# Moving 14 of 93 convolution taps on VectorE to later slots of a hybrid decoder layer

## The chip, the cores and the metric

The kernel runs on one core of a Trainium2 chip. The metric is the device time of one execution in microseconds (us); lower is better. The core has five engines that run side by side and meet only through semaphores: TensorE (PE in the rows, with its weight loads as PEld), VectorE (DVE), ScalarE (ACT), GpSimd (POOL) and SyncE (SP), which issues DMAs.

## The reference

Two layers of a decoder trunk work on 520 tokens: a prompt of 512 and eight decode tokens with state. Each layer has four token mixers beside each other, merged by sigmoid gates, and then a SwiGLU channel mixer:

```
xn = RMSNorm(x)
[A | B | C | D | gates] = xn @ w_in
A: o_a = Bg * dwconv3(Cg * h)
B: o_b = swish(LN(dwconv31(GLU(a, b))))        <- the 31-tap depthwise convolution
C: sliding-window attention (window 128) with QK-norm, rotary and sinks
D: gated linear attention, chunked recurrence
x = x + (sum_r sigmoid(gate_r) * (o_r @ w_branch[r])) @ w_out
x = x + SwiGLU(RMSNorm(x))
```

What matters here is branch B: each of 512 channels is convolved along the tokens with its own 31 weights. The sum for a channel is y[t] = bias + sum over w of weight[w] * u[t + w - 30].

## The kernel before, in words

**Layout.** Channels lie on the 128 partitions and tokens along the free dimension, so 512 channels are four chunks of 128 partitions by 520 tokens. Each fp32 product is made of three fp32r products: every weight tile and every activation tile is split into a rounded part (`whi`, `xhi`, by ScalarE) and the rest (`wlo`, `xlo`, by VectorE), and TensorE adds hi*hi, hi*lo and lo*hi in PSUM.

**Slots.** The input projection, the gates and the branch projections are 103 slots a layer, listed in order in `SLOTS`; a slot makes one output chunk. Those that matter here are numbered from 0:

- 0 to 7: `cfb` and `cfa`, the two inputs of the GLU of branch B. After slot 7 the convolution's input `cfu` is complete.
- 8 to 13: `aq` (four chunks of q), `ak`, `av`, each followed by norm and rotary steps two and four slots later.
- 14 to 25: branch A, as two groups of six: `sch` 14, 15; `scc` 16, 17; `scb` 18, 19; then `sch` 20, 21; `scc` 22, 23; `scb` 24, 25. An `scc` slot holds the whole short convolution of a chunk on VectorE (a chain of nine instructions behind the eviction, each waiting for those before it).
- 26 to 29: the first gates; 30 to 33 the first branch projection, and so on.

The accumulators `acc` are two buffers in turn: the products of slot n + 2 start only when VectorE has taken slot n out of PSUM.

**Order on VectorE.** It runs one fixed program. For each slot n the loop (see below) emits: `side(n)`, the attention or other small work hung on this slot; the `wlo` parts of the weight tiles up to slot n + 2 (line 1269); `evac(n, ...)`, the eviction of the accumulator times `rstd` (line 1260) and, in an `scc` slot, the short convolution (lines 1263, 1556, 1557); and then as many convolution taps as the table `TAPS_AT` gives for n. A tap is one SCALAR_TENSOR_TENSOR of 128 by 512, `cacc <- cfu * weight + cacc` (line 1263). VectorE does chunks 0 to 2, 93 taps: first chunks 0 and 1 in turn, then chunk 2. Since the program is in order, a tap in slot n delays all that VectorE does later: `side(n+1)`, `wlo`, and the eviction of n + 1.

**GpSimd** does chunk 3 by itself from the end of slot 7 on: for each tap a TENSOR_SCALAR into `ssum` (line 1723) and a TENSOR_TENSOR that adds it to `cacc` (line 1726).

**The attention steps on this stretch.** TensorE's own side work follows the products of its slot. At slot 17 (`SATT`) it makes the decode tokens' scores (line 663) from `qz`, which VectorE fills in its `side(17)` (line 1340). At slot 19 it transposes the probabilities `sprob` (line 669), which VectorE finishes in `side(19)` (line 1355) after ScalarE's exponential. The prompt's attention is in eight groups, started at slots `ATT` = 20, 22, 24, 26, 32, ...: scores on TensorE at the end of that slot (line 698), mask and maximum on VectorE in the next slot's side, exponentials on ScalarE, normalisation `prob` on VectorE in the side of the slot after (line 1260), and the transposes of `prob` on TensorE at the end of that slot (line 711), then the values (line 687). So group 1 has its scores in slot 22, its maximum in `side(23)`, its normalisation in `side(24)` and its transposes behind the products of slot 24.

Of the kernel before, what the change touches and what calls it, by code (L numbers as in the profile page):

```python
# [160 lines left out]
TAPS = [(c, w) for w in range(W2) for c in (0, 1)] + [(2, w) for w in range(W2)]  # L161
TAPS_AT = {}
_left = len(TAPS)
for _first, _last, _m in ((4, 7, 3), (8, 9, 4), (10, 17, 2), (20, 21, 2), (29, 29, 2), (30, 33, 1), (34, 37, 2),
                          (38, 41, 1), (42, 53, 3)):
    for _n in range(_first, _last + 1):
        TAPS_AT[_n] = min(_m, _left)
        _left -= TAPS_AT[_n]
# [1729 lines left out]
```

How the kernel before makes its waits and increments, by code:

```python
            def need(self, *points):  # L510
                for name, value in points:
                    self.eng.wait_ge(s[name], value)
# [3 lines left out]
            @block.sync  # L516
            def _(sp):
                for k in range(0, KD, 2):
                    sp.dma_start(x[:, k:k + 2], xt[:, k:k + 2]).then_inc(x_part[k // 2], 16)
                sp.dma_start(raw[:, 0], wt[0]).then_inc(raw_in[0], 16)
                sp.dma_start(raw[:, 1], wt[1]).then_inc(raw_in[1], 16)
                sp.dma_start(cs[:], cst).then_inc(cst_in, 16)
                sp.dma_start(glam[:], glam_d).then_inc(cst_in, 16)
                sp.dma_start(scanm[:], scan_d).then_inc(cst_in, 16)
                sp.dma_start(yt, xt).then_inc(y_out, 16)
                sp.wait_ge(raw_in[1], 16)
# [1 line left out]
            @block.scalar  # L529
            def _(a):
                a.dma_start(gmix[:], gm[0]).then_inc(s["gm_in"], 16)
                a.preload_act_table_set("natural_log_exp_and_others")
                a.wait_ge(s["gm_in"], 16)
                for k in range(KD):
                    if k % 2 == 0:
                        a.wait_ge(x_part[k // 2], 16)
                    nc.scalar.activation(xhi[:, k], x[:, k], ACT.Copy, scale=gmix[:, k:k + 1])\
                        .then_inc(s["xhi_done"], 1)
                    if k >= 2:
                        a.wait_ge(s["ss_done"], k - 1)
                    nc.scalar.activation(tmp[:, k % 2], x[:, k], ACT.Square).then_inc(s["ss_sq"], 1)
                a.wait_ge(raw_in[0], 16)
```

## Time and profile before

| | |
|---|---|
| time, three runs | 2087.36, 2087.77 (median), 2089.17 us |
| the profiled execution | 2088.41 us, of which 2086.4 us are the span from its first to its last instruction |
| mean granted TensorE clock | 0.994 of 2.4 GHz |
| PE, DVE, ACT, POOL busy | 98%, 59%, 38%, 18% of the span |
| slots 8 to 24 of layer 1 | 75.17 to 191.81 us (eviction of 8 to eviction of 24) |
| the same of layer 2 | 1109.34 to 1227.90 us |

The busy share of PE is an upper bound: a matmul that waits for its weights or is pipelined behind another counts as busy. A row of the timeline gives start, duration, engine, line, operation, what it writes and reads, the count when equal ones are merged, and in brackets the idle time before it and who ended it. Two taps that are merged have one start and the sum of their time.

### The profile page before, as it was taken

What the parts mean: (1) busy time and instruction counts of PE and PEld (TensorE: products, weight loads), DVE (VectorE), ACT (ScalarE), POOL (GpSimd) and SP (SyncE); (2) the same over time, 40 slices, a digit from 0 to 9 for tenths busy, and PEclk for the clock granted to TensorE, in tenths of its full rate; (3) what the DMA queues carried; (4) which work ended last, traced back from release to release, by engine and by line L of the source; (5) the groups of instructions that cost most, each with busy time, mean ns of one, the idle gap of its engine ahead of it and who ended that gap; (6) DMA issues with size and microseconds to landing.
All of it is one profiled execution on the core that took longest, in us unless ns stands there. A gap on an engine that the chain in (4) does not pass through costs nothing.

```text
span 2086.4 us, 38895 instructions
## 1 busy us (share of the span) xinstructions
PE 2036.1 (98%) x16516; PEld 1982.0 (95%) x16516; DVE 1225.7 (59%) x1667; ACT 787.3 (38%) x1209; POOL 380.6 (18%) x238
## 2 busy tenths in 40 slices
PE   6989999999999999999989999999999999999998
PEld 6989889999999999999989998899999999999998
DVE  4897667765556453345539975677555565533445
ACT  4323442643543432233233144435535333322332
POOL 0695000211104000000307930003111030000003
PEclk9999999999999999999999999999999999999999
DMA  7523323123222222222444243222223232222223
GB/s 237 97 84 82 71 72 109 67 92 102 105 99 85 98 95 89 99 81 78 139 120 88 91 62 82 73 100 82 94 82 122 82 101 101 75 93 95 101 76 127
DMA packets 70038, 199.54 MB, mean 96 GB/s; under 512 B 41554, under 2 KB 42706, under 8 KB 51408
## 3 DMA queue, kind: packets, MB, share of 16 engines
q1 hardware_dynamic: 26144, 177.50, 25.6%
q10 hardware_dynamic: 43760, 20.11, 5.4%
q8 instruction: 102, 1.67, 0.4%
q14 instruction: 32, 0.26, 0.0%
HBM read 187.42 MB, written 12.29 MB: 96 GB/s over the span
## 4 chain that ended last, share of the span: by engine, by line
PE 43%; DVE 5%; issue 1%; ACT 1%; POOL 0%; DVEq 0%; POOLq 0%
PE acc L604 40%; DVE cacc L1263 1%; DVE wlo L1269 1%; PE m L698 1%; PE m L687 1%; DVE q L1260 1%; ACT tmp L947 0%; DVE sct L1263 0%; PE m L711 0%; PE m L618 0%; DVE gt L1260 0%; PE m L813 0%; PE m L785 0%; PE m L823 0%; PE m L663 0%
## 5 line engine op out<-in xcount | busy, mean ns | idle before, releaser
L604 PE MATMUL acc<-xhi,wlo 128*128 128x260 f32 x3680 | 754.5, 286 | 28.7 <-PEq L567 19.5
L604 PE MATMUL acc<-xhi,whi 128*128 128x260 f32 x3680 | 743.8, 284 | 0.0
L604 PE MATMUL acc<-xlo,whi 128*128 128x260 f32 x3680 | 742.7, 283 | 0.0
L604 PEld LDWEIGHTS acc<-xhi,wlo 128*128 128x128 f32 x3680 | 571.7, 190 | 46.3 <-issue 40.0
L604 PEld LDWEIGHTS acc<-xhi,whi 128*128 128x128 f32 x3680 | 569.6, 189 | 0.0
L604 PEld LDWEIGHTS acc<-xlo,whi 128*128 128x128 f32 x3680 | 569.3, 189 | 0.0
L1269 DVE TENSOR_TENSOR wlo<-raw,whi 128x1024 fp32r<-128x1024 f32 (+3 forms) x344 | 434.4, 1271 | 36.2 <-ACT whi L964 34.8
L964 ACT ACTIVATE whi<-raw 128x1024 fp32r<-128x1024 f32 (+3 forms) x344 | 332.1, 994 | 255.2 <-PE acc L604 197.9
L947 ACT ACTIVATE gt<-gt 128x520 f32<-128x520 f32 x226 | 144.4, 639 | 215.0 <-DVE gt L1260 210.2
L1260 DVE TENSOR_TENSOR gt<-acc,rstd 128x520 f32<-128x520 f32 x80 | 55.9, 699 | 216.0 <-PE acc L604 195.7
L604 PE MATMUL acc<-hhi,whi 128*128 128x260 f32 x704 | 141.5, 282 | 0.0
L604 PE MATMUL acc<-hlo,whi 128*128 128x260 f32 x704 | 141.5, 282 | 0.0
L604 PE MATMUL acc<-hhi,wlo 128*128 128x260 f32 x704 | 141.4, 282 | 0.0
L1263 DVE SCALAR_TENSOR_TENSOR cacc<-cfu,pr,cacc 128x512 f32<-128x512 f32 x180 | 138.2, 794 | 1.6
L1767 POOL TENSOR_TENSOR tmp<-x 128x520 f32<-128x520 f32 x2 | 2.1, 1054 | 656.0 <-DVE x L1686 656.0
L1723 POOL TENSOR_SCALAR ssum<-cfu,pr 128x512 f32<-128x512 f32 x60 | 120.3, 2004 | 5.9
L1654 DVE TENSOR_TENSOR gt<-acc,rstd 128x520 f32<-128x520 f32 x44 | 30.8, 700 | 134.0 <-PE acc L604 122.9
L604 PEld LDWEIGHTS acc<-hlo,whi 128*128 128x128 f32 x704 | 108.4, 188 | 0.0
L604 PEld LDWEIGHTS acc<-hhi,wlo 128*128 128x128 f32 x704 | 108.4, 188 | 0.0
L604 PEld LDWEIGHTS acc<-hhi,whi 128*128 128x128 f32 x704 | 108.3, 188 | 0.0
L604 PE MATMUL acc<-ohi,wlo 128*128 128x260 f32 x512 | 106.9, 290 | 0.5 <-DVE gt L1260 0.4
L604 PE MATMUL acc<-ohi,whi 128*128 128x260 f32 x512 | 103.1, 283 | 0.0
(224 smaller groups left out, 2132.6 us busy)
## 6 DMA issues: line engine op xcount, KB each, us to landing
raw<-in_wt SPq DMA_DIRECT2D x142, 1024.0 KB, 4.8
raw<-in_wt SPq DMA_DIRECT2D x16, 768.0 KB, 4.3
raw<-in_wt SPq DMA_DIRECT2D x16, 640.0 KB, 3.9
x<-yt ACTq DMA_DIRECT2D x2, 2080.0 KB, 9.4
yt<-x ACTq DMA_DIRECT2D x16, 260.0 KB, 2.1
x<-in_xt SPq DMA_DIRECT2D x4, 520.0 KB, 5.0
yt<-in_xt SPq DMA_DIRECT2D x1, 2080.0 KB, 16.1
s<-in_gs ACTq DMA_DIRECT2D x4, 512.0 KB, 3.6
```

The costliest lines, as they stand in the source:

```text
L604: ins = nc.tensor.matmul(out[:, h], a, b[:, h * TH:h * TH + TH], start=first and n == 0, stop=last and n == 2)
L687: ins = nc.tensor.matmul(m4[rows, 2], vb[:, blk - 1 + kc, rows], probt[:, kc], start=kc == k0, stop=kc == 1)
L698: ins = nc.tensor.matmul(m4[:, h // 2, (h % 2) * 256 + k0 * P:(h % 2) * 256 + 256], q[rows, h, blk * P:blk * P + P], kt[rows, (blk - 1 + k ...
L947: return st(nc.scalar.activation(out, in_, func, **kw), name)
L964: nc.scalar.activation(whi[:, ts, 0:length], raw[:, e, off:off + length], ACT.Copy)\
L1260: return st(nc.vector.tensor_tensor(out, in0, in1, op), name)
L1263: return st(nc.vector.scalar_tensor_tensor(out=out, in0=in0, scalar=scalar, in1=in1, op0=op0, op1=op1), name)
L1269: nc.vector.tensor_tensor(wlo[:, ts, 0:length], raw[:, e, off:off + length], whi[:, ts, 0:length].bitcast(F32), ALU.subtract)\
L1654: nc.vector.tensor_tensor(halves(t), acc_of(0), halves(rstd[:]), ALU.mult)\
L1723: st(nc.gpsimd.tensor_scalar(ssum[:, 0:SEQ], cfu[:, c, w:w + SEQ], par_("cc", c * W2 + w), None, ALU.mult))
L1767: nc.gpsimd.tensor_tensor(tmp[:, 0], x[:, 0], x[:, 0], ALU.mult).then_inc(s["ss_sq"], 1)
```

## The change

Only the table that says how many taps stand in which slot changes:

```diff
-for _first, _last, _m in ((4, 7, 3), (8, 9, 4), (10, 17, 2), (20, 21, 2), (29, 29, 2), (30, 33, 1), (34, 37, 2),
-                          (38, 41, 1), (42, 53, 3)):
+for _first, _last, _m in ((4, 7, 3), (8, 17, 1), (20, 29, 2), (30, 33, 1), (34, 37, 2), (38, 41, 1), (42, 53, 3)):
```

| slots | taps a slot before | after |
|---|---|---|
| 8, 9 | 4 | 1 |
| 10 to 17 | 2 | 1 |
| 18, 19 | 0 | 0 |
| 20, 21 | 2 | 2 |
| 22 to 28 | 0 | 2 |
| 29 on | as before | as before |

So 3 + 3 + 8 = 14 taps a layer leave slots 8 to 17, and 7 times 2 arrive in slots 22 to 28; 36 taps are done by slot 17 before, 22 after, and both have 42 done by slot 29. Which tap is done, on which engine and in which order stays. The names keep their lines less one in the changed kernel, since the table is a line shorter.

VectorE's program at the end of slot 16 and in `side(17)`, before (`sct` is the short convolution's chunk, `cacc<-cfu,pr,cacc` a tap, `kts` and `qz` are what TensorE's scores at slot 17 need):

```order
L1263 SCALAR_TENSOR_TENSOR sct<-small,pr,sct 128x8
L1263 SCALAR_TENSOR_TENSOR cacc<-cfu,pr,cacc 128x512 x2
L1337 COPY kts<-kt 128x8
L1340 COPY qz<-q 64x8x4 x2
L1269 TENSOR_TENSOR wlo<-raw,whi 128x1024
```

The same place on VectorE after the change:

```order
L1262 SCALAR_TENSOR_TENSOR sct<-small,pr,sct 128x8
L1262 SCALAR_TENSOR_TENSOR cacc<-cfu,pr,cacc 128x512
L1336 COPY kts<-kt 128x8
L1339 COPY qz<-q 64x8x4 x2
L1268 TENSOR_TENSOR wlo<-raw,whi 128x1024
```

One tap instead of two stands between the short convolution of slot 16 and the copy to `qz`; slot 17's own taps, behind its eviction, shrink in the same way.

VectorE's program at the end of slot 23 and in `side(24)`, before (`prob` is the normalised probability of attention group 1, `small` its sums):

```order
L1263 SCALAR_TENSOR_TENSOR sct<-scu,pr,sct 128x512
L1263 SCALAR_TENSOR_TENSOR sct<-small,pr,sct 128x8
L1260 TENSOR_TENSOR small<-small 128x4
L1387 RECIPROCAL small<-small 128x4
L1260 TENSOR_TENSOR prob<-prob,small 128x4x128
L1269 TENSOR_TENSOR wlo<-raw,whi 128x1024
```

The same place on VectorE after the change:

```order
L1262 SCALAR_TENSOR_TENSOR sct<-scu,pr,sct 128x512
L1262 SCALAR_TENSOR_TENSOR sct<-small,pr,sct 128x8
L1262 SCALAR_TENSOR_TENSOR cacc<-cfu,pr,cacc 128x512 x2
L1259 TENSOR_TENSOR small<-small 128x4
L1386 RECIPROCAL small<-small 128x4
L1259 TENSOR_TENSOR prob<-prob,small 128x4x128
L1268 TENSOR_TENSOR wlo<-raw,whi 128x1024
```

Two taps now stand ahead of the normalisation of `prob`, and in slot 22 two more stand between the short convolution and the maximum of the same attention group.

## Rows read from the trace of the kernel before

**Rows 1.** Chain that ended last, layer 2: start, us, engine, tile, line.

```profile
1172.45 1.15 DVE kts L1337
...
1226.16 0.70 DVE prob L1260
```

**Rows 2.** Waits of PE: waiting line <- what ended it: us in all, times, longest.

```profile
PE m L663 <- DVE qz L1340: 7.2, 2, 3.6
PE m L711 <- DVE prob L1260: 2.9, 4, 1.1
PE m L669 <- DVE sprob L1355: 1.8, 1, 1.8
```

**Rows 3.** Stretches: length, busy by engine (instructions), granted PE clock, DMA.

```profile
75.17:129.75 54.58, 54.58 (x425) 53.40 (x424) 53.51 (x57) 16.79 (x23) 52.03 (x29) 1.00 0.48 83
155.15:176.40 21.25, 21.14 (x174) 20.76 (x174) 16.37 (x26) 5.35 (x13) 20.16 (x13) 1.00 0.29 99
...
1173.90:1189.90 16.00, 15.95 (x112) 15.51 (x112) 14.24 (x24) 3.22 (x6) 15.27 (x9) 0.84 0.39 141
```

**Rows 4.** Timeline of PE, side work of slots 16, 17, 19, 24; last two layer 2.

```profile
129.75 0.60 PE L656 MATMUL m<-cs,vt 128*128 128x128 f32 x4
...
139.75 1.96 PE L663 MATMUL m<-kts,qz 128*64 128x128 f32 x16 [3.56 <-DVE qz L1340]
...
155.26 0.27 PE L669 MATMUL m<-cs,sprob 64*128 64x64 f32 x1 [1.84 <-DVE sprob L1355]
...
190.81 0.66 PE L711 MATMUL m<-cs,prob 128*128 128x128 f32 x4 [0.43 <-DVE prob L1260]
...
1173.95 3.67 PE L663 MATMUL m<-kts,qz 128*64 128x128 f32 x16 [3.59 <-DVE qz L1340]
...
1226.91 0.66 PE L711 MATMUL m<-cs,prob 128*128 128x128 f32 x4 [0.32 <-DVE prob L1260]
```

**Rows 5.** Timeline of DVE, layer 1: slots 16, 17 and then 22 to 24.

```profile
130.72 0.69 DVE L1260 TENSOR_TENSOR tmp<-acc,rstd 128x520 f32<-128x520 f32 x1
...
136.84 1.41 DVE L1263 SCALAR_TENSOR_TENSOR cacc<-cfu,pr,cacc 128x512 f32<-128x512 f32 x2
138.17 1.23 DVE L1337 COPY kts<-kt 128x8 f32<-128x8 f32 x1
...
176.41 0.69 DVE L1260 TENSOR_TENSOR tmp<-acc,rstd 128x520 f32<-128x520 f32 x1
...
190.07 0.69 DVE L1260 TENSOR_TENSOR prob<-prob,small 128x512 f32<-128x512 f32 x1
```

**Rows 6.** Timeline of DVE, layer 1: idle places in slots 24 to 28.

```profile
193.94 0.70 DVE L1260 TENSOR_TENSOR olo<-sct,ohi 128x520 fp32r<-128x520 f32 x1 [0.71 <-ACT ohi L947]
...
199.37 0.70 DVE L1260 TENSOR_TENSOR tmp<-acc,rstd 128x520 f32<-128x520 f32 x1 [0.67 <-PE acc L604]
...
206.32 0.70 DVE L1260 TENSOR_TENSOR gt<-acc,rstd 128x520 f32<-128x520 f32 x1 [1.43 <-PE acc L604]
209.12 1.29 DVE L1263 SCALAR_TENSOR_TENSOR prob<-m,cs 128x512 f32<-128x512 f32 x2 [2.09 <-PE m L698]
...
222.87 0.70 DVE L1260 TENSOR_TENSOR gt<-acc,rstd 128x520 f32<-128x520 f32 x1 [4.41 <-PE acc L604]
```

**Rows 7.** Timelines of DVE and POOL: taps beside GpSimd's chunk.

```profile
1104.99 2.07 DVE L1263 SCALAR_TENSOR_TENSOR cacc<-cfu,pr,cacc 128x512 f32<-128x512 f32 x3
1109.95 4.22 DVE L1263 SCALAR_TENSOR_TENSOR cacc<-cfu,pr,cacc 128x512 f32<-128x512 f32 x4
1110.43 1.42 POOL L1726 TENSOR_TENSOR cacc<-cacc,ssum 128x512 f32<-128x512 f32 x1
...
124.04 2.26 DVE L1263 SCALAR_TENSOR_TENSOR cacc<-cfu,pr,cacc 128x512 f32<-128x512 f32 x2
...
135.59 2.07 POOL L1723 TENSOR_SCALAR ssum<-cfu,pr 128x512 f32<-128x512 f32 x1
...
184.88 1.61 POOL L1726 TENSOR_TENSOR cacc<-cacc,ssum 128x512 f32<-128x512 f32 x1
```

## The prediction, made before the changed kernel ran

> **What bounds the kernel now.** I read the chain of waits first. In layer 2 it runs on TensorE up to slot 7, on VectorE from slot 8 to the copies for `qz` in slot 17, then on TensorE, and again on VectorE through slots 22 and 23 to the normalisation `prob` ahead of line 711 [rows 1]. That looks as if VectorE bounded all of slots 8 to 17. The busy time by stretch corrects it: from the eviction of slot 8 to the end of slot 16's products VectorE is busy 53.5 of 54.6 us, but TensorE is busy for the whole 54.6 at full clock [rows 3], and in its timeline no gap stands there. VectorE runs about one slot behind and TensorE does not feel it, because two accumulators are in turn. The list of TensorE's waits says where it does feel it: at line 663 (slot 17), 3.6 us in each layer; at line 669 (slot 19), 1.8 us in one layer; and at line 711, where the first of four small waits is the one in slot 24 [rows 2]. The timeline of TensorE places them: 3.56 and 1.84 us in layer 1 and 0.43 us in slot 24; 3.59 and 0.32 us in layer 2, with none at line 669 [rows 4]. So what counts is the moment at which `qz`, `sprob` and `prob` of group 1 are ready, and nothing between.
>
> **What the removed taps give.** Twelve of the 14 taps that leave (slots 8 to 15) lie in the stretch where TensorE has no gap. At 0.66 us a tap (two taps from 136.84 to 138.17 [rows 5]) that is 7.9 us of VectorE and no TensorE time; it only lets VectorE catch up. Slot 16's eviction began at 130.72 [rows 5], though its products were done at 129.75, when line 656 starts [rows 4]: at most 0.97 us of lag to win, of which I take 0.9, since an eviction follows the products by a little anyway. The slot 16 tap stands directly ahead of `qz`: 0.66 us more. So `qz` comes 1.5 us earlier and the wait at line 663 shrinks from 3.56 to 2.0 us. It can't shrink below zero, so the other end is 3.56; at the low end VectorE is held by one of GpSimd's adds more than before, 1.42 us [rows 7], and the gain is 0.1.
>
> From `qz` to `sprob` VectorE goes through slot 17's eviction, short convolution and taps; one tap less is again 0.66 us. In layer 1, where line 669 waits for it, the transposes there come 1.5 + 0.66 = 2.2 us earlier; the wait falls from 1.84 to about 1.1 us. In layer 2 line 669 does not wait: the granted clock is 0.84 over the 16.0 us between [rows 3], so TensorE itself is late by 0.16 x 16.0 = 2.6 us, and line 663 alone takes 3.67 us there against 1.96 in layer 1 [rows 4]. If the clock does the same again, the gain is 1.5 us. If not, VectorE's chain ends last as in layer 1, where line 663 to line 669 took 155.26 - 139.75 = 15.5 us; less 0.66 it is 14.85, against 15.95 in layer 2, and the gain is 2.6 us. I take 1.5, the clock as it was.
>
> From line 669 on TensorE is busy 21.1 of 21.25 us up to the eviction of slot 22 [rows 3], so the gain is carried there whole: 2.2 us in layer 1, 1.5 in layer 2.
>
> **What the added taps cost.** From the eviction of slot 22 (176.41) VectorE works through short convolution, maximum of group 1, eviction and short convolution of slot 23, to `prob` at 190.07 + 0.69 = 190.76 [rows 5], and line 711 starts at 190.81 after a wait [rows 4]. There is no cover left: TensorE already waits for this chain in both layers, and it began with a slot that TensorE had just finished. Slots 22 and 23 now put two taps each into it: 4 x 0.66 = 2.65 us. GpSimd's chunk still runs during slot 22 (its last add ends at 184.88 + 1.61 = 186.5, ten us after that slot's eviction [rows 7]), and a tap can be held by it: two taps took 2.26 us in slot 15 instead of 1.41 [rows 5, 7]. Of the 20 two-tap groups beside GpSimd's chunk in both layers three were held so, one by 0.2 us, so I add 0.15: 2.8 us. The ends: both groups held, 2.65 + 1.7 = 4.4 us; below, one of GpSimd's adds fewer is in VectorE's way in slot 22, 2.65 - 1.42 = 1.2 us.
>
> The other ten taps, in slots 24 to 28, cost nothing. Slots 24 and 25 add 2 x 1.33 us; VectorE is idle there 0.71 us before each of two `olo` (one is shown) and 0.67 before the eviction of 25, together 2.1, and 1.43 more before the eviction of 26 [rows 6]. Behind slot 26 it is idle 2.09 us, and behind 27 4.41 us [rows 6], each more than the 1.33 that comes. If that cover were gone, each slot would cost up to 1.33 us. From slot 29 on nothing differs.
>
> The Trainium skill ("SBUF — State Buffer", section "Who interferes with whom") says that a VectorE instruction with two SBUF inputs and a GpSimd instruction that reads SBUF exclude each other for the whole of the instruction. The trace agrees for GpSimd's adds: four taps took 4.22 us, where three alone take 2.07, which is 1.46 us over 4 x 0.69, with an add of 1.42 us in their midst [rows 7]. It does not for GpSimd's multiply, which reads SBUF too: the two taps from 136.84 on took 1.41 us while one ran from 135.59 to 137.66 [rows 5, 7]. By the rule each of the added pairs would wait through an add as well as a multiply; by the rows only an add can hold it.
>
> **The sum.** Layer 1: -2.2 + 2.8 = +0.6 us. Layer 2: -1.5 + 2.8 = +1.3 us. Together +1.9 us on the profiled execution's 2088.4 us, which lies 0.6 us above the median of the runs; against that median of 2087.8 it is 2089.7 us. A measurement here can tell about 0.2%, 4.2 us, from no change: the forecast is no measurable change. TensorE's wait moves from slots 17 and 19 to slot 24, where it becomes 0.43 + 2.8 = 3.2 us.
>
> **Rivals.**
> 1. *Slower: the clock falls behind the new wait.* The price is not the wait but what follows it. In layer 2 the wait of 3.59 us at line 663 was followed by half-rate matmuls (1.2 of 2.4 GHz), 2.6 us in all as above; in layer 1 one of 3.56 us was not [rows 3, 4]. The new wait of 3.2 us at line 711 is nearly as long. If the clock falls there in one layer, 1.9 + 2.6 = 4.5 us, 2092.3; in both, 7.1 us, 2094.9. It decides as soon as one layer loses it without layer 2's slot 17 winning it back. For it: one of two such waits had it. Against it: waits of 1.84 us did not, and the shorter wait in slot 17 may end the fall there, which gives 2.6 - 1.5 = 1.1 us back. Chance 0.16.
> 2. *Slower: GpSimd holds the added taps.* Both pairs held in both layers: 1.9 + 2 x (4.4 - 2.8) = 5.1 us, 2092.9. For it: GpSimd runs there. Against it: only three of 20 pairs were held. The rule above, taken as it stands, would make it the usual case. Chance 0.05.
> 3. *Faster: GpSimd gets out of the way.* With VectorE less busy in slots 8 to 15 GpSimd's chunk may end some us sooner, and `qz` is not held. Then the wait of 3.56 us goes whole, `sprob` comes 3.56 + 0.66 = 4.2 us earlier in layer 1, and slots 22 and 23 pay the low end of 1.2. Layer 1: -4.2 + 1.2 = -3.0; layer 2: -3.56 + 1.2 = -2.4; together -5.4 us, 2082.4. Against it: the slot 22 chain begins earlier too, so GpSimd is about as far as before when it starts. Chance 0.12.
> 4. *No wait moves, layer 2 warm at slot 17:* +0.8 us, 2088.6. Chance 0.12.
>
> **Chances and range.** The forecast itself has 0.55. Same, within 0.2%: 0.55 + 0.12 = 0.67; slower 0.16 + 0.05 = 0.21; faster 0.12. The range is 2084.5 to 2094.5: up to nearly both layers of rival 1, and down to some two thirds of the way from no change to rival 3. The worst ends of all bounds at once, in both layers, are left out.
>
> **What would show it.** Line 663 waits about 2.0 us instead of 3.6; line 669 about 1.1 in layer 1; line 711's longest wait grows to about 3.2 us in both layers, at slot 24; VectorE's idle time appears in slots 8 to 15; from slot 25 on the timeline is the old one shifted by less than 2 us a layer. I am wrong on slot 17 if line 663 still waits over 3 us or not at all; on slots 22 to 24 if line 711 waits under 1.5 us; on the clock if slots 24 and 25 have a granted clock under 1.0; and on the cover if line 711 waits in slot 26 or 28.

## The result and the profile after

The changed kernel took 2097.44 us (median of six runs, 2095.45 to 2097.68); the kernel before took 2087.77 beside it (2086.55 to 2089.17). The ratio is 1.0044, with a 95% interval from 1.0033 to 1.0054: slower by 9 us, twice what a measurement of this kernel can tell from no change. The forecast of 2089.7 us and its range up to 2094.5 were wrong. The profiled execution took 2097.47 us, with a span of 2095.6 and a mean granted clock of 0.992 (before: 2088.41, 2086.4 and 0.994).

In the changed kernel every line number from the table on is one lower: what was line 711 is 710, 663 is 662, 669 is 668, 698 is 697, 687 is 686. The waits of PE of the changed kernel (waiting line <- what ended it: us in all, times, longest) answer to [rows 2]:

```profile
PE m L710 <- DVE prob L1259: 10.1, 4, 3.9
...
PE m L662 <- DVE qz L1339: 3.9, 2, 2.0
PE m L668 <- DVE sprob L1354: 2.3, 2, 1.1
```

The two waits that were to shrink did so by the amounts forecast: 2.0 us at the line of `qz`, 1.1 at that of `sprob`. The wait for `prob` grew to 3.9 where 3.2 was forecast. The waits alone come out close, and yet the time does not. PE's timeline of the changed kernel (start, us, line, shapes, wait in brackets), which answers to [rows 4], shows what comes behind the waits; the rows of the second half are layer 2:

```profile
137.40 1.96 PE L662 MATMUL m<-kts,qz 128*64 128x128 f32 x16 [1.95 <-DVE qz L1339]
...
152.20 0.27 PE L668 MATMUL m<-cs,sprob 64*128 64x64 f32 x1 [1.13 <-DVE sprob L1354]
...
172.76 0.60 PE L710 MATMUL m<-cs,prob 128*128 128x128 f32 x4
...
191.27 1.11 PE L710 MATMUL m<-cs,prob 128*128 128x128 f32 x4 [3.94 <-DVE prob L1259]
192.31 3.78 PE L697 MATMUL m<-kt,q 64*128 64x256 f32 x8
...
1177.79 1.96 PE L662 MATMUL m<-kts,qz 128*64 128x128 f32 x16 [1.97 <-DVE qz L1339]
...
1192.60 0.27 PE L668 MATMUL m<-cs,sprob 64*128 64x64 f32 x1 [1.14 <-DVE sprob L1354]
...
1231.65 1.11 PE L710 MATMUL m<-cs,prob 128*128 128x128 f32 x4 [3.94 <-DVE prob L1259]
1232.70 3.78 PE L697 MATMUL m<-kt,q 64*128 64x256 f32 x8
```

Behind the wait the four transposes take 1.11 us where they took 0.66 [rows 4], and the scores of line 697, which take 1.99 us at full clock, take 3.78. The same work in the kernel before, from the transposes in slot 24 to line 687 in slot 25, took 8.45 us at full clock in both layers (stretch: length, busy time by engine, granted clock, DMA share, GB/s):

```profile
190.81:199.26 8.45, 8.45 (x60) 7.64 (x60) 7.04 (x11) 2.78 (x9) 0.00 (x0) 1.00 0.01 3
1226.91:1235.36 8.45, 8.45 (x60) 7.64 (x60) 7.04 (x11) 2.79 (x9) 0.00 (x0) 1.00 0.01 3
```

After the change the same matmuls take 12.63 and 12.94 us, busy throughout, at a granted clock of 0.64 and 0.62. The third row is the stretch of slots 8 to 16, which answers to the first of [rows 3]:

```profile
191.27:203.90 12.63, 12.63 (x60) 10.96 (x60) 8.37 (x13) 4.25 (x12) 0.00 (x0) 0.64 0.17 62
1231.65:1244.59 12.94, 12.94 (x61) 11.26 (x61) 8.37 (x13) 4.25 (x12) 0.00 (x0) 0.62 0.22 73
...
74.42:129.00 54.58, 54.58 (x424) 53.40 (x423) 42.86 (x45) 16.79 (x23) 51.95 (x30) 1.00 0.51 83
```

The chain of waits in layer 2 (start, us, engine, tile, line) now passes through the tap pair of slot 23 to `prob`, and from there to TensorE; [rows 1] had `prob` at the same place:

```profile
1229.18 1.41 DVE cacc L1262 x2
...
1230.91 0.70 DVE prob L1259
...
1231.65 1.11 PE m L710 x4
```

**The ledger.** In layer 1 line 710 of slot 24 starts 191.27 - 190.81 = 0.46 us later than before; slot 8 had started 0.75 sooner, so the slots between cost 1.2. In layer 2 it is 1231.65 - 1226.91 = 4.74 later, and TensorE had come into slot 9 5.46 late (the eviction of slot 8 starts at 1114.80 instead of 1109.34), so they gave 0.7. Then follow 12.63 - 8.45 = 4.18 us and 12.94 - 8.45 = 4.49 us of lost clock. What lies ahead of slot 8 and between the layers, -0.75 and +0.8, cancels. 1.2 - 0.7 + 4.18 + 4.49 = 9.2 us is the whole difference of the spans, 2095.6 - 2086.4. The +0.8 between the layers holds one more fall of the clock: from 505 to 520 us TensorE is busy throughout in both kernels, at a granted clock of 1.00 before and 0.89 after, which costs 1.7 us. TensorE has no gap from 490 to 505 us either, so no wait stands just ahead of it, and what brought it stays open.

VectorE and GpSimd in slots 16, 22 and 23 (their timelines, which answer to [rows 5, 7]; the two taps of slot 22 stand one by one):

```profile
129.20 0.70 DVE L1259 TENSOR_TENSOR tmp<-acc,rstd 128x520 f32<-128x520 f32 x1 [0.98 <-PE acc L603]
...
134.74 1.80 DVE L1262 SCALAR_TENSOR_TENSOR cacc<-cfu,pr,cacc 128x512 f32<-128x512 f32 x1
136.47 0.16 DVE L1336 COPY kts<-kt 128x8 f32<-128x8 f32 x1
...
178.78 1.82 DVE L1262 SCALAR_TENSOR_TENSOR cacc<-cfu,pr,cacc 128x512 f32<-128x512 f32 x1
180.53 1.17 DVE L1262 SCALAR_TENSOR_TENSOR cacc<-cfu,pr,cacc 128x512 f32<-128x512 f32 x1
...
188.79 1.41 DVE L1262 SCALAR_TENSOR_TENSOR cacc<-cfu,pr,cacc 128x512 f32<-128x512 f32 x2
...
178.77 1.29 POOL L1725 TENSOR_TENSOR cacc<-cacc,ssum 128x512 f32<-128x512 f32 x1
180.16 1.88 POOL L1722 TENSOR_SCALAR ssum<-cfu,pr 128x512 f32<-128x512 f32 x1
182.12 1.29 POOL L1725 TENSOR_TENSOR cacc<-cacc,ssum 128x512 f32<-128x512 f32 x1
```

Slot 16's eviction now waits for TensorE (0.98 us idle): VectorE has caught up. Slot 22's pair takes 2.92 us from its first start to its last end. Its first tap starts 0.01 us after one of GpSimd's adds (178.77 to 180.06) and ends only behind it, after 1.82 us, where a tap of slot 23 takes 0.75; its second takes 1.17 us beside GpSimd's next multiply (180.16 to 182.04). In layer 2 the pair takes 2.92 us too. Slot 23's pair takes 1.41, with GpSimd's chunk over by 183.4.

### The profile page after: what moved, and what is told of

It is laid out like the page before. It is cut to its first block, busy times and chain, and to the rows that moved or that the text cites. A ratio compares the mean times of both kernels' runs of the same rounds, so it can differ in the third digit from the quotient of the medians.

```text
span 2095.6 us, 38897 instructions
## 1 busy us (share of the span) xinstructions
PE 2040.5 (97%) x16516; PEld 1984.6 (95%) x16516; DVE 1219.8 (58%) x1667; ACT 787.7 (38%) x1209; POOL 376.3 (18%) x238
## 4 chain that ended last, share of the span: by engine, by line
PE 45%; DVE 3%; issue 1%; ACT 1%; POOL 0%; ACTq 0%; POOLq 0%; DVEq 0%
PE acc L603 41%; PE m L697 1%; PE m L686 1%; DVE wlo L1268 0%; ACT tmp L946 0%; DVE sct L1262 0%; PE m L710 0%; DVE cacc L1262 0%; PE m L617 0%; PE m L647 0%; PE m L636 0%; PE m L812 0%; PE m L784 0%; PE m L822 0%; PE m L772 0%
```

## The experiments

Theory A: the added taps in slots 22 and 23 make `prob` late, TensorE waits for it, and the price is paid twice, as the wait and as the half rate behind it. The rivals lay the time to the tap table's other parts, to GpSimd, or to something else than TensorE's pause. The tables below move taps and leave none out; the times of the kernel before beside them were 2087.3 to 2087.7 us. Each run's rows carry the line numbers of its own kernel: some are numbered as before (711), some as the changed kernel (710), and with the wait filled line 710 is 714.

**Only 22 and 23.** The kernel before with two taps a slot in 20 to 23 and two in 8 and 9; no other slot of the region of 10 to 23 is changed.

```diff
-(8, 9, 4), (10, 17, 2), (20, 21, 2), (29, 29, 2)
+(8, 9, 2), (10, 17, 2), (20, 23, 2), (29, 29, 2)
```

> The table of before, with four taps taken from slots 8 and 9 (two each) and put into slots 22 and 23 (two each); all else as before. Theory A (the four taps lengthen VectorE's chain to prob, TensorE then idles nearly 4 us ahead of the transposes of attention group 1 at the end of slot 24, and its clock falls to 1.2 GHz behind that): line 663 still waits 3.6 us, line 711 about 3.5 to 4.5 us in both layers, granted clock about 0.62 to 0.65 from there to the end of slot 25's products, some 7 us a layer, about 2102 us. Rival B (the loss comes from the ten taps in slots 24 to 28, or from the stretch 8 to 17): no loss here, 2087 to 2089. Rival C (the wait alone, the clock keeps): about 2094.

Measured: 2101.03 us, ratio 1.0065 [1.0049, 1.0081]. PE at line 711 in slot 24 of layers 1 and 2:

```profile
193.69 1.12 PE L711 MATMUL m<-cs,prob 128*128 128x128 f32 x4 [3.94 <-DVE prob L1260]
...
1235.53 0.66 PE L711 MATMUL m<-cs,prob 128*128 128x128 f32 x4 [2.44 <-DVE prob L1260]
```

The wait is 3.94 in layer 1, as expected, and 2.44 in layer 2, where 3.5 to 4.5 was expected as well, and the half rate stands behind both (12.37 and 11.59 us up to line 687, where 8.45 is full rate). These four taps alone cost more than the whole change.

**None in 22 and 23.** The changed kernel without these four taps; slots 26 and 27 take four each.

```diff
-(20, 29, 2)
+(20, 21, 2), (24, 25, 2), (26, 27, 4), (28, 29, 2)
```

> The changed table, but slots 22 and 23 without taps; their four taps stand in slots 26 and 27, which have four each. Theory A: the shorter waits at slots 17 and 19 stay (2.0 and 1.1 us), line 711 in slot 24 waits under 0.6 us, the clock stays at 2.4 GHz, and the time is below before: about 2082 (2.3 us less in layer 1, 4.3 in layer 2 up to slot 22, give or take 1). Rival B (taps in slots 24 to 28 cost): 2093 or more. Rival C (wait alone, clock not a matter of the wait): 2088 to 2090.

Measured: 2082.09 us, ratio 0.9976 [0.9965, 0.9987]: faster than both kernels. PE's timeline in slots 24 and 25 of layer 1:

```profile
187.45 0.65 PE L711 MATMUL m<-cs,prob 128*128 128x128 f32 x4 [0.41 <-DVE prob L1260]
188.04 1.99 PE L698 MATMUL m<-kt,q 64*128 64x256 f32 x8
...
195.90 1.07 PE L687 MATMUL m<-probt,vb 128*64 128x512 f32 x2
```

The wait is 0.41 us, the scores take 1.99, and line 687 comes 8.45 us behind. So thinning 8 to 17 does pay, and slots 22 and 23 are what turns the change around.

**One tap in 22 and one in 23.**

```diff
-(20, 29, 2)
+(20, 21, 2), (22, 23, 1), (24, 25, 2), (26, 27, 3), (28, 29, 2)
```

> The changed table with one tap each in slots 22 and 23 in place of two; the other two stand in slots 26 and 27, three each. Line 711 should wait about 1.7 us, up to 3 if GpSimd holds the tap of slot 22. Theory A, where the clock falls only behind a long wait: if the wait is about 2 us or less the clock keeps and the time is 2084 to 2087; the loss is not half of the change's. Rival D (loss in proportion to the taps): halfway between the two-tap and the no-tap table, about 2089 to 2090, with a half-rate stretch half as long.

Measured: 2093.42 us (2086.33 to 2095.09 over ten runs), ratio 1.002 [1.0009, 1.003]. The wait is 3.07 us, more than half of 3.94, because slot 22's single tap was held by GpSimd's add as well (1.81 us). The clock falls behind it in both layers of the profile. The expected way to a kept clock, a wait of 2 us or less, did not come about here. The runs of this one kernel lie 9 us apart, against 2 to 3 us of the kernel before and of the changed one in the first comparison; the two fastest have mean clocks of 0.994 and 0.995, the slower ones 0.991 to 0.993. The program is the same each time, so it looks as if the clock that goes with the wait varies; only one of the ten runs has a trace, a slower one, so that is not shown.

**Scores ahead of the wait.** The changed kernel, with line 697's scores of the next group issued in slot 24 before the transposes that wait.

```diff
-for g in range(NBLK * NKV):
+for g in (reversed(range(NBLK * NKV)) if n == ATT[2] else range(NBLK * NKV)):
```

> The changed kernel, but at the end of slot 24 TensorE makes the scores of attention group 2 (line 698) before it waits for prob of group 1, in place of after; VectorE's program is untouched. The wait for prob shrinks by the scores' 1.9 us to about 2 us, and prob comes no sooner. Theory A (the length of the idle time brings the clock down): clock keeps, time falls by 2 x (1.9 + 4.3) to about 2085. Rival E (the transposes and half-array scores are too little work for the clock whatever the wait): half-rate stretch stays, only 2 x 1.9 us are won, about 2093.5.

Measured: 2086.89 us, ratio 1.0000 [0.9991, 1.001], 10.5 us under the changed kernel. The scores fill 1.99 us of the wait and 2.01 are left; a shorter half rate still follows it (slot 25's products take 7.21 and 8.27 us where full rate is 6.0). So the time is near theory A's 2085, but its reason is only half of it: the clock is not kept, as rival E had it, and what is won is the wait that the scores fill and the scores' own full rate (1.99 instead of 3.78 us).

**The wait filled.** The changed kernel, with eight matmuls of ones by a table of cosines into a bank that nobody reads, in front of the transposes in slot 24.

```diff
+if n == ATT[2]:
+    pe.wait_ge(s["a_max"], 2)
+    for i in range(8):
+        nc.tensor.matmul(m4[:, i % 2, 0:TH], ones, cosm[:, 0:TH], start=True, stop=True)
```

> The changed kernel, with eight matmuls more (ones by a table of cosines, into a bank that nobody reads) in front of L710 in slot 24, so that TensorE has work while it waits for prob. Theory A (a wait of 3.94 us is paid once as a wait, 0.65 us per layer more than forecast, and a second time as the half rate that follows it, 4.2 and 4.5 us): prob is ready as late as before, L710 starts at the same distance from slot 22, but the scores behind it take 2.0 instead of 3.78, slot 25's products 5.9 instead of 8.0, and the time falls by 8 to 9 us to about 2088.5 (2087 to 2090). Rival B (the slow stretch comes from what DVE or GpSimd do, or from the scores' own operands, and not from TensorE's pause): no change, 2096 to 2098.

Measured: 2086.98 us, ratio 0.9997 [0.9988, 1.0007]. PE's timeline in slots 22 and 24 of layer 1, and then the stretches behind the wait in both layers (columns as above):

```profile
172.52 0.60 PE L714 MATMUL m<-cs,prob 128*128 128x128 f32 x4
...
186.92 3.67 PE L692 MATMUL m<-cs 128*128 128x260 f32 x16
191.01 0.66 PE L714 MATMUL m<-cs,prob 128*128 128x128 f32 x4 [0.42 <-DVE prob L1263]
```

```profile
191.01:199.46 8.45, 8.45 (x60) 7.64 (x61) 8.28 (x13) 2.25 (x7) 0.00 (x0) 1.00 0.01 3
1225.47:1233.92 8.45, 8.45 (x60) 7.64 (x60) 8.28 (x13) 2.25 (x7) 0.00 (x0) 1.00 0.01 3
```

This is the run that separates the two prices. `prob` is as late as in the changed kernel: the transposes (line 714 here) start 191.01 - 172.52 = 18.49 us behind those of slot 22, there 191.27 - 172.76 = 18.51. But TensorE was at work in the meantime, and the 8.45 us of full clock are back in both layers. That is 4.18 + 4.49 = 8.7 us of the 10.5 between the medians; the other 1.8 lie between the two layers, where the changed kernel's clock of 0.89 from 505 to 520 us is 1.00 in this run, which is 1.7 us.

**GpSimd out of the way.** The changed kernel with three of the 30 taps that GpSimd adds up for chunk 3 left out in each layer, so that its values there are incomplete.

```diff
-for w in range(1, W2):
+for w in range(1, W2 - 3):
```

> The changed kernel, with three of the 30 taps of GpSimd's third chunk left out in each layer (its values are then incomplete), so that GpSimd's adds end about when slot 22 starts, some 8 us sooner. Theory A (the wait of L710 is VectorE's late prob, and 1.5 us of it come from the add on GpSimd that holds slot 22's two taps; the half rate follows the wait): slot 22's taps take 1.41 each instead of 2.92, prob is ready 1.3 to 1.5 us sooner or more, L710 waits 2.0 to 2.6 instead of 3.94, and the time is 2.6 us lower by the two waits alone, near 2094.5, and near 2086 if the half rate goes with them. Rival B (GpSimd has nothing to do with slot 22's length): slot 22's taps stay at 2.9, the wait at 3.9, the time at 2097.

Measured: 2082.95 us, ratio 0.9978 [0.9967, 0.999], some 3 us under what was expected. Slot 22 on VectorE and slot 24 on PE:

```profile
176.96 1.42 DVE L1262 SCALAR_TENSOR_TENSOR cacc<-cfu,pr,cacc 128x512 f32<-128x512 f32 x2
...
187.80 0.66 PE L710 MATMUL m<-cs,prob 128*128 128x128 f32 x4 [0.86 <-DVE prob L1259]
188.38 1.99 PE L697 MATMUL m<-kt,q 64*128 64x256 f32 x8
```

The pair takes 1.42 us, as expected. The wait fell by 3.1 us where 1.3 to 1.9 were expected: GpSimd's adds hold the small operations of slot 22's short convolution as well, and had done so in the kernel before (the one of 128 x 8 elements that takes 1.27 us there, from 178.34 on, takes 0.23 here). No half rate follows 0.86 us.

**Four taps in 23.** The changed kernel with slot 22's pair moved behind the end of GpSimd's chunk.

```diff
-(20, 29, 2)
+(20, 21, 2), (23, 23, 4), (24, 29, 2)
```

> The changed kernel with slot 22's two taps moved to slot 23, where GpSimd's chunk is over: four taps there, none in 22. Without taps in both slots L710 waits 0.41; four unheld taps are 4 x 0.66 = 2.65 more, so 3.05 instead of 3.94. Theory A (wait plus a fall of the clock behind it, whatever the taps' slot): the wait saves 0.9 a layer, the clock still falls as it did behind a wait of 3.07, time near that kernel's 2093.5. Rival (the price is GpSimd's hold, not the wait): without the hold no half rate, 2087 or less.

Measured: 2095.32 us, ratio 1.0044 [1.0028, 1.0061]. VectorE in slot 23 and PE in slot 24:

```profile
186.06 2.74 DVE L1262 SCALAR_TENSOR_TENSOR cacc<-cfu,pr,cacc 128x512 f32<-128x512 f32 x4
...
189.87 1.12 PE L710 MATMUL m<-cs,prob 128*128 128x128 f32 x4 [3.08 <-DVE prob L1259]
```

No tap is held, the wait is the 3.08 us expected, and the half rate is as long as ever (13.10 us up to line 686, in both layers). So the hold on the taps is not what brings the half rate; it only lengthens the wait.

**Two taps in 23, none in 22.**

```diff
-(20, 29, 2)
+(20, 21, 2), (23, 23, 2), (24, 25, 2), (26, 26, 4), (27, 29, 2)
```

> The changed kernel with two taps in slot 23, none in 22, the other two in slot 26. L710 waits 0.41 + 2 x 0.66 = 1.7. A wait of 0.86 was followed by no half rate and one of 3.07 by it in both layers; one of 2.0 with scores of 1.9 ahead of it was too. If 1.7 is short enough: 2082.1 of the kernel without taps in both slots, plus 2 x 1.33 = 2084.8. If the clock falls as behind 2.0: some 2089.

Measured: 2089.97 us, ratio 1.0014 [1.0004, 1.0024]. PE in slots 24 and 25 of layer 1:

```profile
188.59 0.66 PE L710 MATMUL m<-cs,prob 128*128 128x128 f32 x4 [1.74 <-DVE prob L1259]
189.17 3.09 PE L697 MATMUL m<-kt,q 64*128 64x256 f32 x8
...
200.16 1.07 PE L686 MATMUL m<-probt,vb 128*64 128x512 f32 x2
```

The clock falls behind a wait of 1.74 us too, and behind 1.62 in layer 2 (11.57 and 11.56 us up to line 686), and the time is near the 2089 expected for that case. Two unheld taps of 0.66 us in each layer cost 7.9 us against the table without them.

**Only 16 and 17 thinned**, in the kernel before.

```diff
-(8, 9, 4), (10, 17, 2), (20, 21, 2), (29, 29, 2)
+(8, 9, 4), (10, 15, 2), (16, 17, 1), (20, 21, 2), (27, 27, 2), (29, 29, 2)
```

> The kernel before, with slots 16 and 17 thinned from two taps to one, slot 27 taking the two that come free, and nothing else moved. My steps: slots 16 and 17 lie where TensorE waits for qz (L663) and sprob (L669), so these two taps are worth 0.66 each: L663's wait falls from 3.56 to about 2.9, L669's from 1.84 to about 1.8 (its lag is qz's own and only one tap lies between), TensorE gains some 1.3 us a layer at slot 20, time near 2085. Rival: DVE's lag from slots 8 to 15 is what delays qz, then L663 waits 3.3 or more.

One run: 2087.33 us, no measurable gain. The wait for `qz` is 2.94 us instead of 3.56, as expected, but layer 2 keeps its slow clock behind it, and the wait for `sprob` grew from 1.84 to 2.14 where 1.8 was expected. Layer 1 loses what it won: from line 669 to the first line 711 TensorE takes 22.06 us at a clock of 0.92, where the kernel before takes 20.56 at 1.00. PE at line 663 in layers 1 and 2:

```profile
138.71 1.96 PE L663 MATMUL m<-kts,qz 128*64 128x128 f32 x16 [2.94 <-DVE qz L1340]
...
1173.23 2.41 PE L663 MATMUL m<-kts,qz 128*64 128x128 f32 x16 [2.91 <-DVE qz L1340]
```

**Only 8 to 15 thinned**, in the table without taps in 22 and 23.

```diff
-(8, 17, 1), (20, 29, 2)
+(8, 15, 1), (16, 17, 2), (20, 21, 2), (24, 25, 2), (26, 27, 4), (29, 29, 2)
```

> The changed kernel with two taps in 16 and 17 as before, one a slot in 8 to 15, none in 22 and 23. My steps: thinning 8 to 15 gives only the lag that DVE carries out of the stretch, 0.9 us at L663: wait 2.7 there instead of 3.56, 1.84 or less at L669, time near 2085. Rival: thinning 8 to 15 gives all of the gain at L663 (wait 2.0) or none (3.5).

One run: 2093.64 us, a miss of 9 us. The wait for `qz` is 2.87 us (2.7 expected), but the one for `sprob` is 3.84. VectorE in slots 16 and 17, and PE at line 669:

```profile
134.75 2.90 DVE L1263 SCALAR_TENSOR_TENSOR cacc<-cfu,pr,cacc 128x512 f32<-128x512 f32 x2
...
145.82 2.92 DVE L1263 SCALAR_TENSOR_TENSOR cacc<-cfu,pr,cacc 128x512 f32<-128x512 f32 x2
...
155.82 0.27 PE L669 MATMUL m<-cs,sprob 64*128 64x64 f32 x1 [3.84 <-DVE sprob L1355]
```

Both pairs are now held by one of GpSimd's adds; in the kernel before neither was (1.41 us in slot 16 [rows 5], 1.42 in slot 17). The clock fell behind line 669 in both layers. The two parts of the change in 8 to 17 are not additive: when VectorE has caught up, its taps fall on other moments of GpSimd's chunk.

**None in 16, 17, 22 and 23**, with two taps a slot in 8 and 9, as a version to beat both.

```diff
-(8, 17, 1), (20, 29, 2)
+(8, 9, 2), (10, 15, 1), (20, 21, 2), (24, 25, 2), (26, 27, 4), (28, 29, 2)
```

> No taps in slots 16, 17, 22 and 23, one a slot in 10 to 15: a version that should beat both kernels. By the steps, two taps of 0.66 to 0.71 less ahead of qz and of sprob: L662 waits 0.6 to 1.3 instead of 1.95, L668 0.5 to 1.1 instead of 1.13, L710 0.4 to 0.6 as with nothing in 22 and 23; 1.0 to 1.5 us a layer under the version without taps in 22 and 23 alone, 2079 to 2081. Rival: the two more taps in 8 and 9, or the qz chain itself and not the taps, set L662's wait: it stays at 1.9 and the time at 2082.

Measured: 2080.94 us, ratio 0.9975 [0.9965, 0.9986]. The wait for `qz` is 0.94 us in layer 1 and 0.93 in layer 2, inside the expectation. The wait for `sprob` is 1.40, over it. Beside 0.9976 of the table without taps in 22 and 23 alone the difference can't be told. Both beat the kernel before by 5 to 7 us.

Put together, by the wait in slot 24 (layer 1 / layer 2) and the time from those transposes to line 686 or 687 in slot 25, 8.45 us at full clock, both from the profiled execution, beside the median of all runs:

| kernel | wait, us | to slot 25's line 686/687, us | median, us |
|---|---|---|---|
| before | 0.43 / 0.32 | 8.45 / 8.45 | 2087.8 |
| none in 22, 23 | 0.41 / 0.38 | 8.45 / 8.45 | 2082.1 |
| GpSimd shorter | 0.86 / 0.89 | 8.44 / 8.44 | 2083.0 |
| two taps in 23 | 1.74 / 1.62 | 11.57 / 11.56 | 2090.0 |
| one tap in 22, one in 23 | 3.07 / 3.08 | 11.63 / 11.61 | 2093.4 |
| four in 23 | 3.08 / 3.08 | 13.10 / 13.10 | 2095.3 |
| changed kernel | 3.94 / 3.94 | 12.63 / 12.94 | 2097.4 |
| only 22 and 23 | 3.94 / 2.44 | 12.37 / 11.59 | 2101.0 |
| changed, wait filled | 0.42 / 0.40 | 8.45 / 8.45 | 2087.0 |
| none in 16, 17, 22, 23 | 0.43 / 0.28 | 8.44 / 8.45 | 2080.9 |

## Why the prediction was wrong

**The failed step: the clock behind the new wait was counted at nothing.** The prediction's sum held the wait alone, +0.6 and +1.3 us; the half rate stood in rival 1, with a chance of 0.16 and 2.6 us a layer. It came in both layers and cost 4.18 and 4.49, so that even the rival's 2094.9 for both layers was 2.5 us short. The sign that the prediction had named for it, a clock under 1.0 in slots 24 and 25, is there: 0.64 and 0.62. The reason for the low chance was that of two like waits at line 663, in layers 1 and 2, only one had been followed by half rate. That place was the wrong witness. Line 663 goes on being followed by half rate in layer 2 alone, behind 3.59, 3.27, 2.91 and 2.85 us in four kernels; behind slot 24's wait the clock fell in both layers of every profile in which it was 1.6 us or more. The price was taken from the same wrong place.

**Slots 22 and 23, 2.8 us a layer: undersized.** The four taps took 2.92 + 1.41 = 4.33 us in both layers; other small operations were held less, and the wait grew by 3.94 - 0.43 = 3.5 in layer 1. The 0.15 us for GpSimd's hold was an average over 20 pairs, four of which had been longer (2.26, 2.27, 2.31 and 1.63 us). An average is the wrong measure here: whether a pair is held is set by where GpSimd's adds stand when VectorE comes to it, and that was the same in both layers. The pair in slot 22 could be held or not, 1.5 us apart; in layer 2 of the run with 22 and 23 alone, where TensorE came at another moment, it took 1.42. The rule of the Trainium skill ("SBUF — State Buffer", section "Who interferes with whom") would have made the hold the usual case, and for this pair it came true. The prediction's "only an add can hold it" was too narrow: slot 22's second tap took 1.17 us instead of 0.75 with nothing of GpSimd's beside it but a multiply (180.16 to 182.04). The multiply did not hold it to its end, though, and the pair of [rows 5] was not held by one at all. Rival 3 did not come: GpSimd's chunk ended 3.1 us sooner than before (183.4 instead of 186.5), but slot 22 began 3.1 us sooner too (173.35 instead of 176.41), as the prediction had held against it.

**Slot 17, wait 3.56 to 2.0: right.** It is 1.95 and 1.97. Its two terms, 0.9 for the lag and 0.66 for the tap, were 0.69 and 0.62 in the runs of each alone. In the changed kernel their sum comes out with some luck: the one tap left in slot 16 is held and takes 1.80 us, more than the pair did before (1.41 [rows 5]), while the copy to `kts` behind it, held before (1.23 us [rows 5]), is free now (0.16). The prediction had a term for neither hold, and the two cancel.

**Slot 19: right in layer 1, undersized in layer 2.** The wait is 1.13 where 1.1 was forecast. In layer 2 the prediction took a gain of 1.5 us, "the clock as it was"; with the wait at 1.97 the clock stayed full there (1.96 us for line 662, 3.67 before [rows 4]) and slot 22 came 4.3 us sooner, more than the upper bound of 2.6, since another half-rate stretch of the kernel before in slots 20 and 21 went as well. The prediction had carried the gain from line 669 to slot 22 by layer 1's row alone; these are both layers of the kernel before, from line 669 to the first line 711 (columns as in the stretches above):

```profile
155.26:175.82 20.56, 20.56 (x169) 20.35 (x170) 15.68 (x25) 5.35 (x13) 19.47 (x13) 1.00 0.30 103
1189.93:1212.03 22.10, 22.10 (x171) 21.89 (x171) 14.97 (x25) 5.35 (x13) 20.93 (x14) 0.92 0.28 96
```

Rival 4 had layer 2 at full clock at slot 17 and gave 1.1 us for it; it was worth 2.8. So the clock was misjudged twice: it gave 2.8 us more than forecast here and took 8.7 there.

**Cover in slots 24 to 28: right.** Of the 4.41 us of idle time ahead of slot 28's eviction [rows 6] 3.08 are left, of the 1.43 ahead of slot 26's 0.91, and line 710's two other waits, in later slots, stay at 1.1 us. With the wait filled, where no lost clock gives VectorE time, the same two rows read 3.08 and 0.89. VectorE's timeline after the change:

```profile
210.97 0.70 DVE L1259 TENSOR_TENSOR gt<-acc,rstd 128x520 f32<-128x520 f32 x1 [0.91 <-PE acc L603]
...
227.51 0.70 DVE L1259 TENSOR_TENSOR gt<-acc,rstd 128x520 f32<-128x520 f32 x1 [3.08 <-PE acc L603]
```

**Slots 8 to 15 give nothing by themselves: right.** TensorE is busy 54.58 of 54.58 us there before and after, while VectorE's share went from 53.5 to 42.9.

**What stays open.** Why line 663 loses the clock in layer 2 and never in layer 1, behind waits that agree within 0.05 us and after stretches that are alike (54.6 us of full work at clock 1.00 in both layers). And why 1.95 us at line 662 brings no half rate while 1.74 us at line 710 does; different matmuls stand behind the two waits, and no run exchanged them. A wait just ahead is not needed either: in layer 2 of the kernel before the clock falls in slots 20 and 21 (0.92 over the 22.10 us above), and TensorE had last waited at line 663, 16 us before that stretch begins. The same fall of some 1.5 us stands in layer 2 of three tables whose layer 1 has none there (only 22 and 23; two taps in 23; none in 16, 17, 22 and 23). So the runs show that the new wait in slot 24 brings its half rate, since filling it takes the half rate away, and do not show a rule for when the clock falls.

## What to carry to other kernels

A new wait of TensorE can have two prices, its length and the clock behind it, and here the second was the larger (4.18 and 4.49 us against 3.5 and 3.6): ask of every new wait what it costs if the stretch behind it runs at half rate, and where the trace has no such wait at that place, take neither the chance nor the price of it from another. Work that is put off belongs where TensorE does not wait for the engine; just ahead of a producer that it already waits for, two taps of 0.66 us in each layer cost 7.9 us in all. Where nothing can be moved, filling the wait with matmuls that nobody needs gave 10 us back here; not having it gave 15.

## What was not expected of the hardware

- A wait of 1.62 to 1.74 us, after 6 us of unbroken products at full rate, was followed by 0.70 of the full clock over 11.6 us.
- The length of the half rate does not follow that of the wait: 3.08 us cost 3.2 us in one kernel (11.63) and 4.65 in another (13.10).
- GpSimd's adds hold not only the taps: the small operation of 128 x 8 elements in slot 22's short convolution takes 1.27 us with one of GpSimd's adds beside it and 0.23 without, as these rows of the changed kernel and of the run with the shorter chunk show.

```profile
175.28 1.27 DVE L1556 TENSOR_SCALAR sct<-small,pr 128x8 f32<-128x8 f32 x1
...
174.95 1.56 POOL L1725 TENSOR_TENSOR cacc<-cacc,ssum 128x512 f32<-128x512 f32 x1
```

```profile
174.85 0.23 DVE L1556 TENSOR_SCALAR sct<-small,pr 128x8 f32<-128x8 f32 x1
```
